# A two-block network on one core: in its second kind of layer the attention heads' values become the stationary operand, two heads share a bank by halves, and each head's probabilities are scaled before they are turned

## The chip, the core and the metric

The kernel runs on one core of a Trainium2 chip. The metric is the device time of one execution in microseconds (us). A core has a matmul engine, TensorE (PE in the profile; PEld is its weight load), VectorE (DVE), ScalarE (ACT), GpSimd (POOL) and SyncE (SP), which here only starts transfers. The engines run on their own and meet at semaphores. TensorE writes its results to eight banks of PSUM, 128 partitions by 512 numbers of 32 bits each.

## The reference, cut to what matters

`x` has 256 rows of 1024 numbers. Two layers of a first kind come first, then two layers of a second kind; the change touches the second kind alone. A layer of the second kind, shortened:

```python
h = rms_norm_2(x, g_mix)
(a_q, a_k, a_v, b_qlat, b_kvlat, b_krope, c_q, c_k, c_v, c_f, d_val, d_gate) = jnp.split(h @ w_in, ...)
out_a = chunk_band_attention(...)            # 4 heads of 64, a bias by distance, masked by chunks of 64
q = (rms_norm_2(b_qlat, g_q_lat) @ w_uq)     # the "latents": 256 and 128 numbers a row
kv = (rms_norm_2(b_kvlat, g_kv_lat) @ w_ukv)
out_b = block_causal_attention(...)          # 4 heads of 96 (values 64), with a rotation of q and k
out_c = block_causal_attention(...)          # 4 heads of 64, with a cumulated forget term
out_d = silu(layer_norm(conv(d_val * sigmoid(d_gate))))   # 31 taps
# in each head: p = softmax(scores); out = p @ v   (256 queries, 256 keys, 64 values; keys behind a query only)
proj = einsum('bsnc,ncd->bsnd', [out_a, out_b, out_c, out_d], w_branch)   # 4 branches of 256
x = x + sum(sigmoid(h @ w_gate + b_gate) * proj) @ w_o
x = x + square(relu(rms_norm_2(x, g_ffn) @ w_up)) @ w_down
```

## The kernel before

**The large products.** Weights come from memory in *slabs* of four blocks of 128 x 512 (some of two or one). ScalarE rounds a slab to `w_hi` (L1066) and VectorE takes the rest to `w_lo` (L1588); activations are split alike. Each product is three matmuls, hi by hi, hi by lo and lo by hi (L513 to L515). VectorE and ScalarE work three slabs ahead of TensorE. A product gathers in one of two pairs of banks (0 and 1, or 2 and 3). They are taken in turn by *block number*: block n waits in `open_block` until block n-2 has been read out.

**The attention beside them.** The heads of the second kind (0 to 3 are `out_a`, 4 to 7 `out_c`, 8 to 11 `out_b`) are worked on in steps. Each engine has a generator `side()`, and the table `PLAN2` says after which slab a step of it is taken. It is the same table for all engines, so the order on each is fixed by hand. In step h TensorE makes the scores of head h (`head_scores`, L847 and L848, into bank 6), turns q and k of a later pair of heads for h from 4 to 9 (`turn_head`), turns the probabilities of head h-1 (`turn_probs`) and makes the outputs of head h-2 (`head_values`, L870 to L872). Turning is a transpose on TensorE against the identity `cst` (L559 for all), into bank 4 or 5 in turn, and ScalarE copies the result out.

VectorE adds the bias and finds the rows' maxima (`soften`, L1919 to L1925), and ScalarE takes the exponentials and their sums (`exponentials`, L1385). The probabilities stay unscaled. Both have a 128 x 128 piece for the first 128 queries and a 128 x 256 piece for the others.

**The heads' outputs.** `head_values(h)` has the turned probabilities `softT2` as the stationary operand, 128 x 128, and 64 columns of values as the moving one, three matmuls in f32. Four heads fill bank 7, queries in the partitions. Then VectorE divides by the sums and writes `branch` (`normalise`, L1933 and L1936), TensorE turns `branch` with four transposes (`turn_branch`), ScalarE rounds the result to `obT_hi` and VectorE takes `obT_lo`; the products with `w_branch` (named B0 to B7) read these two. The convolution's branch goes through `turn_branch` as well. This happens for branch 0 (heads 0 to 3), 1 (4 to 7), 2 (8 to 11) and 3 (convolution).

**The latents' products.** U0 and U1 (the products with `w_uq` and `w_ukv`) stand behind gate product G0. U0 takes banks 0 and 1, and then a block number is left out, so that the number of blocks in a layer is even. U1 therefore takes banks 0 and 1 too, when ScalarE has read U0 out. At the end of the layer a number of the turning banks is left out as well. GpSimd rotates parts of q and k for heads 8 to 11 behind U1 (L2272 to L2285).

A matmul of f32 operands shows as two records in the trace, each with its own weight load; a transpose, and a matmul of the rounded operands, shows as one.

Of the kernel before, what the change touches and what calls it, by code (L numbers as in the profile page):

```python
# [21 lines left out]
F32 = mybir.dt.float32  # L22
# [6 lines left out]
P = 128  # L29
# [37 lines left out]
BLOCKS1, BLOCKS2 = 7 + 2 + 11 + 2, 5 + 2 + 16 + 2 + UPS + 2 + 1  # L67
TURNS1, TURNS2 = 4 + 4 + 4 + 4 + 4 + 4 + 4 + 11 + 4 + 1, 2 + 1 + 1 + 10 + 12 + 4 + 1 + 4 + 4 + 4 + 1
assert not (BLOCKS1 % 2 or BLOCKS2 % 2 or TURNS1 % 2 or TURNS2 % 2)
# [71 lines left out]
STEPS_DVE1, STEPS_DVE2 = 27, 87  # L141
# [51 lines left out]
def build(nc, t, out):  # L193
    with ExitStack() as ctx:
# [140 lines left out]
        probs = sem("probs")  # L335
        heads_out = sem("heads_out")
        decay_arg = sem("decay_arg")
# [154 lines left out]
        def _(pe):  # L492
# [329 lines left out]
            q.next("probs", DEPTH * DH)  # L822
            for l in q.layers(dict(slab=len(KTS2), blk=BLOCKS2, turn=TURNS2, scores=12, pool=2, dve=6, hid=UPS,
                                          probs=12, conv=1, out=3),
                              dict(turn=3)):
# [29 lines left out]
                def head_values(h):  # L855
                    pe.wait_ge(turn_free, group["probs", h] + 2)
                    if h % 4 == 0:
                        pe.wait_ge(out_free, q.next("out"))
                    if h == 0:
                        read_out(projection[3])  # L860
                    s = softT2[:, h % 2, :]

                    def v(kt):
# [40 lines left out]
                def side():  # L904
# [22 lines left out]
                    turn_branch(0)  # L927
# [6 lines left out]
                    turn_branch(2)  # L934
# [7 lines left out]
                    turn_branch(3)  # L942
# [23 lines left out]
                for name in PRODUCTS:  # L966
# [3 lines left out]
                    elif name[0] == "U":  # L970
                        pe.wait_ge(turn_free, group["latents"] + 2)
                        product(open_block(), lat_hi, lat_lo, ((0, 1), (2,))[n], (384, 512)[n], True, True)
                        if n == 0:
                            q.next("blk")
                    else:
                        pe.wait_ge(turn_free, group["branch", n // 2] + 2)
# [52 lines left out]
                for b in range(2):  # L1029
                    a = open_block()  # L1030
                    for n in range(8):
# [6 lines left out]
                        if b == 1 and n == 1 and l < DEPTH - 1:  # L1038
                            turn_added(skip=1)
# [3 lines left out]
        def _(act):  # L1043
# [296 lines left out]
            per2 = dict(slab=len(KTS2), used=len(KTS2), blk=BLOCKS2, turn=TURNS2, soft=12, act_job=1,  # L1340
                        rstd=4, squares=5, conv=1, hid=UPS, step=STEPS_ACT2,
                        **{f"in{s}": 16 * len(KTS2) // RING for s in range(RING)})
            for l in q.layers(per2, dict(slab=AHEAD, turn=3, **{f"in{s}": 16 for s in range(AHEAD)})):
# [12 lines left out]
                def take_block(dst, cols, scales, n, blocks=1):  # L1356
# [6 lines left out]
                    ins.then_inc(acc_free, blocks)  # L1363
                    q.next("blk", blocks - 1)
# [45 lines left out]
                def heads(first, end):  # L1410
                    for h in range(first, end + 2):
                        if h == 10:
                            take_hi(obT_hi[0][:, :, :])
# [18 lines left out]
                def side():  # L1432
# [15 lines left out]
                    take_hi(obT_hi[0][:, :, :])  # L1448
# [4 lines left out]
                    take_hi(obT_hi[1][:, :, :])  # L1453
# [25 lines left out]
                def latent_product(n):  # L1479
# [3 lines left out]
                    take_block(dst, (384, 512)[n], lat[n], 1, 2 - n)  # L1483
# [62 lines left out]
                if l < DEPTH - 1:  # L1546
                    take_model((0, 1), l * 16 + 48)
                    take_model((2, 3), l * 16 + 48, skip=1)
# [22 lines left out]
        def _(dve):  # L1571
# [320 lines left out]
            for l in q.layers(dict(slab=len(KTS2), used=len(KTS2), row=1, blk=BLOCKS2, turn=TURNS2,  # L1892
                                          turn_hi=2 + 4 + 4 + 4 + 4, squares=5, rstd=4, act_done=10, hid=UPS, scores=12,
                                          heads=3, layer_in=64, bgate0=64, bgate1=64, step=STEPS_DVE2),
                              dict(slab=AHEAD, turn=3, turn_hi=2)):
# [15 lines left out]
                def lo_of(dst, hi):  # L1911
                    dve.wait_ge(turn_free, q.now("turn") + 2)
                    take_lo(dst, hi)

# [13 lines left out]
                def normalise(n):  # L1928

                    dve.wait_ge(heads_out, q.next("heads"))  # L1930
                    rs, rc = (stat[:, at:at + 24].rearrange("p (r h) -> p r h", r=R)[:, :, 4 * n:4 * n + 4]
                              for at in (S_RS2, S_RC2))
                    step(dve.reciprocal(rc, rs))  # L1933
                    for r in range(R):
                        at = S_RC2 + 12 * r + 4 * n
                        ins = dve.tensor_tensor(branch[:, r, :].rearrange("p (h d) -> p h d", d=HD),  # L1936
# [397 lines left out]
```

## Time and profile before

| | |
|---|---|
| three runs, median (lowest to highest) | 1453.38 us (1453.35 to 1453.61) |
| the profiled execution | 1453.64 us |
| its span, first to last instruction | 1451.9 us |
| TensorE busy | 1438.1 us, 99% |
| VectorE, ScalarE, GpSimd busy | 932.0, 747.5, 98.4 us |
| mean granted clock of TensorE | 0.998 of 2.4 GHz |

1.7 us of the profiled time lie outside the span. The two layers of the second kind take the second half: their attention stands at about 665 to 810 us and again some 401 us later, with the same pattern. On TensorE a record's duration says little, since matmuls overlap in its pipeline. What one costs is the distance between the *starts* of neighbouring rows of the timeline; this is how the rows below are to be read.

### The profile page before, as it was taken

The page shows a single profiled execution, that of the slowest core. Times are in us where ns is not written, and L with a number is a line of the kernel's source. Part 1 is how long each engine was busy: PE and PEld are TensorE (multiplying, and loading weights), DVE is VectorE, ACT ScalarE, POOL GpSimd, SP SyncE. Part 2 cuts the span into 40 slices and gives each one's busy share as a digit, 9 for nine tenths or more (in the row PEclk, how much of TensorE's full clock was granted, in tenths as well). Part 3 has the DMA queues.
Part 4 walks back from the last instruction along what each step waited for, and adds up shares of the span by engine and source line. Part 5 has one row for each costly group of instructions (what it writes and reads, how often), then busy time and mean ns, then how long its engine had stood idle before and what let it go on. Part 6 is the DMA issues. An engine that isn't in the chain of part 4 may idle for free.

```text
span 1451.9 us, 19158 instructions
## 1 busy us (share of the span) xinstructions
PE 1438.1 (99%) x7099; PEld 1201.0 (83%) x7099; DVE 932.0 (64%) x1111; ACT 747.5 (51%) x994; POOL 98.4 (7%) x116
## 2 busy tenths in 40 slices
PE   9999999999999999999999999999999999999997
PEld 7788888888788888888888888888888888888886
DVE  6766655446756555446688878754466888787642
ACT  6765544445855444346665446543366654565441
POOL 1211000002111000000220000000002200000001
PEclk9999999999999999999999999999999999999999
DMA  8533665555435665555454566555553545665550
GB/s 333 173 123 112 231 189 190 177 183 164 149 109 170 205 186 176 182 180 186 138 177 160 187 206 211 191 193 183 174 186 118 187 160 182 217 204 190 188 186 29
DMA packets 172646, 257.12 MB, mean 177 GB/s; under 512 B 8477, under 2 KB 90399, under 8 KB 172447
## 3 DMA queue, kind: packets, MB, share of 16 engines
q1 hardware_dynamic: 169408, 249.36, 51.5%
q10 hardware_dynamic: 3023, 6.28, 1.4%
q8 instruction: 46, 0.75, 0.2%
q0 software_dynamic: 144, 0.52, 0.1%
q14 instruction: 25, 0.20, 0.0%
HBM read 255.08 MB, written 1.05 MB: 176 GB/s over the span
## 4 chain that ended last, share of the span: by engine, by line
PE 95%; DVE 2%; ACT 1%; issue 1%; DMA 0%; POOL 0%; POOLq 0%; DVEq 0%; ACTq 0%
PE bank L513 23%; PE bank L515 23%; PE bank L514 23%; PE bank L1002 8%; PE bank L559 5%; PE bank L1001 4%; PE bank L697 1%; PE bank L542 1%; PE bank L544 1%; PE bank L543 1%; PE bank L848 1%; DVE w_lo L1588 1%; PE bank L654 1%; PE bank L1004 1%; PE bank L847 1%
## 5 line engine op out<-in xcount | busy, mean ns | idle before, releaser
L1588 DVE TENSOR_TENSOR w_lo<-w_raw,w_hi 128x2048 fp32r<-128x2048 f32 (+2 forms) x247 | 538.6, 2185 | 217.4 <-ACT w_hi L1066 214.3
L1066 ACT CAST w_hi<-w_raw 128x2048 fp32r<-128x2048 f32 (+2 forms) x247 | 448.5, 1825 | 218.5 <-PE bank L515 194.7
L513 PE MATMUL bank<-w_hi,hT 128*128 128x512 f32 (+1 forms) x1056 | 417.5, 395 | 0.0
L515 PE MATMUL bank<-w_hi,hT 128*128 128x512 f32 (+1 forms) x1056 | 410.7, 389 | 0.0
L514 PE MATMUL bank<-w_lo,hT 128*128 128x512 f32 (+1 forms) x1056 | 410.0, 388 | 0.0
L515 PEld LDWEIGHTS bank<-w_hi,hT 128*128 128x128 f32 x1056 | 198.2, 188 | 41.2
L513 PEld LDWEIGHTS bank<-w_hi,hT 128*128 128x128 f32 x1056 | 198.4, 188 | 39.2 <-issue 1.5
L514 PEld LDWEIGHTS bank<-w_lo,hT 128*128 128x128 f32 x1056 | 198.6, 188 | 37.9
L1002 PE MATMUL bank<-hT,w_hi 128*128 128x512 f32 x512 | 178.2, 396 | 0.2
L1001 PE MATMUL bank<-hT,w_lo 128*128 128x256 f32 x448 | 125.2, 279 | 0.0
L2213 POOL TENSOR_TENSOR stat<-stat,cst 128x2 f32<-128x2 f32 (+4 forms) x24 | 46.4, 1935 | 967.4 <-DVE stat L1637 830.7
L1002 PEld LDWEIGHTS bank<-hT,w_hi 128*128 128x128 f32 x512 | 94.4, 188 | 21.0 <-DVE sum L2143 0.9
L513 PE MATMUL bank<-w_hi,hid2T_hi 128*128 128x512 f32 x240 | 93.5, 390 | 0.0
L515 PE MATMUL bank<-w_hi,hid2T_lo 128*128 128x512 f32 x240 | 93.4, 389 | 0.0
L514 PE MATMUL bank<-w_lo,hid2T_hi 128*128 128x512 f32 x240 | 93.4, 389 | 0.0
L1001 PEld LDWEIGHTS bank<-hT,w_lo 128*128 128x128 f32 x448 | 84.4, 188 | 1.3
L513 PE MATMUL bank<-w_hi,hid1T_hi 128*128 128x512 f32 x176 | 69.1, 392 | 0.0
L515 PE MATMUL bank<-w_hi,hid1T_lo 128*128 128x512 f32 x176 | 68.6, 390 | 0.0
L514 PE MATMUL bank<-w_lo,hid1T_hi 128*128 128x512 f32 x176 | 68.5, 389 | 0.0
L1089 ACT CAST hid1T_hi<-bank 128x512 f32 (+1 forms) x22 | 12.9, 587 | 90.3 <-PE bank L559 90.3
L1617 DVE SCALAR_TENSOR_TENSOR hT<-bank,gcols,hT 128x256 fp32r<-128x256 f32 (+1 forms) x72 | 32.6, 507 | 40.8 <-ACT hT L1096 35.5
L1525 ACT COPY cross<-bank 128x256 f32<-128x256 f32 x64 | 20.8, 378 | 70.7 <-PE bank L1002 70.7
(277 smaller groups left out, 1630.5 us busy)
## 6 DMA issues: line engine op xcount, KB each, us to landing
w_raw<-in_w_gate SPq DMA_DIRECT2D x108, 512.0 KB, 3.8
w_raw<-in_w_up SPq DMA_DIRECT2D x108, 512.0 KB, 4.6
w_raw<-in_w_down SPq DMA_DIRECT2D x104, 512.0 KB, 4.5
w_raw<-in_w_in SPq DMA_DIRECT2D x88, 512.0 KB, 4.6
w_raw<-in_w_out SPq DMA_DIRECT2D x16, 512.0 KB, 4.1
w_raw<-in_w_branch SPq DMA_DIRECT2D x32, 256.0 KB, 2.8
w_raw<-in_w_o SPq DMA_DIRECT2D x16, 512.0 KB, 4.5
bgate<-in_b_gate ACTq DMA_DIRECT2D x16, 256.0 KB, 3.3
```

What stands on the lines that cost most here:

```text
L513: pe.matmul(o, hi[:, kt, rows_of(r)], w_hi[:, s, j, 0:cols], start=begin, stop=False)
L514: pe.matmul(o, hi[:, kt, rows_of(r)], w_lo[:, s, j, 0:cols], start=False, stop=False)
L515: mm = pe.matmul(o, lo[:, kt, rows_of(r)], w_hi[:, s, j, 0:cols], start=False, stop=end)
L542: pe.matmul(a[r][:, :], hT_hi[:, kt, rows_of(r)], w_hi[:, s, j, :], start=begin, stop=False)
L559: tr = pe.transpose(b[0:m, col:col + n], src, ident[0:n, 0:n])
L1001: pe.matmul(o[:, 0:SEQ], lo[:, kt, cols], hT_hi[:, kt, :], start=False, stop=False)
L1002: mm = pe.matmul(o[:, :], hi[:, kt, cols], hT[:, :, kt, :], start=kt == 0, stop=kt == KT - 1)
L1066: act.copy(w_hi[:, s, 0:kts, :], w_raw[:, s, 0:kts, :]).then_inc(hi_ready, 1)
L1525: ins = act.copy(cross2[:, n, :], a[n][:, SEQ:2 * SEQ])
L1588: dve.tensor_tensor(w_lo[:, s, 0:kts, :], w_raw[:, s, 0:kts, :], w_hi[:, s, 0:kts, :].bitcast(F32), ALU.subtract).then_inc(lo_ready, 1)
L1617: return dve.scalar_tensor_tensor(lo, src, gain, hi.bitcast(F32), ALU.mult, ALU.subtract)
L2213: pool.tensor_tensor(dst, src, half[:, 0:n], ALU.pow).then_inc(rstd_ready, 1)
```

## The change

Four edits, all in layers of the second kind.

1. `head_values` becomes `pair_values`, taken at every odd step for two heads. The values of a head, 128 x 64, are stationary and the turned probabilities move: 256 columns for the first 128 keys (all queries) and 128 columns for the others (later queries). The even head of a pair writes partitions 0 to 63 of bank 7 and the odd one partitions 64 to 127. So bank 7 holds the branch already turned, and `turn_branch` is gone for the three attention branches; ScalarE (`take_branch`) and VectorE (`lo_of_branch`) read bank 7 itself. The convolution's branch is still turned (`turn_conv`).
2. Queries now lie along the columns, so a head can't be divided by its sums behind the product. `scale_probs` (VectorE) multiplies the probabilities before they are turned, one head at a time: a reciprocal and two `tensor_scalar`. `turn_probs` waits for it (`scaled` in place of `probs`). It stands behind the step's slab split, for head 3 ahead of `latents`. `normalise` is gone.
3. In a step `pair_values` stands ahead of `turn_probs`; `head_values` stood behind it.
4. No block number and no turning number is left out: U1 takes banks 2 and 3, and all later blocks the other pair than before.

```diff
-BLOCKS1, BLOCKS2 = 7 + 2 + 11 + 2, 5 + 2 + 16 + 2 + UPS + 2 + 1
+BLOCKS1, BLOCKS2 = 7 + 2 + 11 + 2, 5 + 2 + 16 + 2 + UPS + 2
...
                 def turn_probs(h):
-                    pe.wait_ge(probs, q.next("probs"))
+                    pe.wait_ge(scaled, q.next("scaled"))
...
-                    o = [score[1][:, r * BW + (h % 4) * HD:r * BW + (h % 4 + 1) * HD] for r in range(R)]
-                    pe.matmul(o[0], s[:, 0:P], v(0), start=True, stop=True)
-                    pe.matmul(o[1], s[:, P:2 * P], v(0), start=True, stop=False)
-                    mm = pe.matmul(o[1], s[:, 2 * P:3 * P], v(1), start=False, stop=True)
+                    for kt, at, n in ((0, 0, SEQ), (1, 2 * P, P)):
+                        for e in range(2):
+                            mm = pe.matmul(score[1][e * HD:(e + 1) * HD, (c + 1) * SEQ - n:(c + 1) * SEQ],
+                                           v(h - 1 + e, kt), softT2[:, e, at:at + n], start=kt == 0, stop=kt == 1)
...
-                def turn_branch(n):
-
-                    pe.wait_ge(out_free, q.now("out") + 1)
-                    group["branch", n] = turn_group([(branch[:, r, c * P:(c + 1) * P], c * SEQ + r * P)
-                                for c in range(2) for r in range(R)])
...
                     for h in range(first, end + 2):
-                        if h == 10:
-                            turn_branch(1)
                         if h < end:
                             head_scores(h)
                             if 4 <= h < 10:
                                 turn_head(h)
+                        if h >= first + 2 and h % 2:
+                            pair_values(h - 2)
                         if first < h <= end:
                             turn_probs(h - 1)
-                        if h >= first + 2:
-                            head_values(h - 2)
...
                         product(open_block(), lat_hi, lat_lo, ((0, 1), (2,))[n], (384, 512)[n], True, True)
-                        if n == 0:
-                            q.next("blk")
...
+                def take_branch(dst):
+
+                    act.wait_ge(heads_out, q.next("heads"))
+                    act.copy(dst[:, :, :], score[1][:, :].rearrange("p (c n) -> p c n", n=SEQ)).then_inc(branch_hi, 1)
...
-                def normalise(n):
-
-                    dve.wait_ge(heads_out, q.next("heads"))
-                    rs, rc = (stat[:, at:at + 24].rearrange("p (r h) -> p r h", r=R)[:, :, 4 * n:4 * n + 4]
-                              for at in (S_RS2, S_RC2))
-                    step(dve.reciprocal(rc, rs))
...
+                def scale_probs(h):
+
+                    dve.wait_ge(probs, q.next("probs"))
+                    rs, rc = (stat[:, at:at + 24].rearrange("p (r h) -> p r h", r=R)[:, :, h] for at in (S_RS2, S_RC2))
+                    step(dve.reciprocal(rc, rs))
+                    for r, (a, z) in enumerate(((0, P), (P, 3 * P))):
+                        ins = dve.tensor_scalar(soft2[:, h % 2, a:z], soft2[:, h % 2, a:z], rc[:, r:r + 1], None, ALU.mult)
+                    ins.then_inc(scaled, 1)
...
+                def lo_of_branch(n):
+
+                    dve.wait_ge(branch_hi, q.next("branch_hi"))
+                    dve.tensor_tensor(obT_lo[n][:, :, :], score[1][:, :].rearrange("p (c n) -> p c n", n=SEQ),
+                                      obT_hi[n][:, :, :].bitcast(F32), ALU.subtract).then_inc(out_free, 1)
...
                     if s not in (12, 38):
                         splits(1)
+                    while softened:
+                        scale_probs(softened.pop(0))
                     if s >= TAPS_FROM:
```

TensorE's queue in step 3 of the first attention, before (scores of head 3, probabilities of head 2 turned, outputs of head 1; bank 7 takes the outputs):

```order
L847 MATMUL bank6<-qkT2_77 128x128 [waits turn_free,scores_out]
L848 MATMUL bank6<-qkT2_77 128x256
L559 MATMUL bank5<-cst,soft2_78 128x128 [waits turn_free,probs]
L559 MATMUL bank5<-cst,soft2_78 128x128 x2
L870 MATMUL bank7<-p_b_65,softT2_79 128x64 [waits turn_free]
L871 MATMUL bank7<-p_b_65,softT2_79 128x64
L872 MATMUL bank7<-p_b_65,softT2_79 128x64
```

And with the change (the outputs are those of heads 0 and 1; line 874 is the matmul in `pair_values`):

```order
L848 MATMUL bank6<-qkT2_77 128x128 [waits turn_free,scores_out]
L849 MATMUL bank6<-qkT2_77 128x256
L874 MATMUL bank7<-softT2_79,p_b_65 64x256 [waits acc_free,out_free,turn_free]
L874 MATMUL bank7<-softT2_79,p_b_65 64x256
L874 MATMUL bank7<-softT2_79,p_b_65 64x128 x2
L561 MATMUL bank5<-cst,soft2_78 128x128 [waits turn_free,scaled]
L561 MATMUL bank5<-cst,soft2_78 128x128 x2
```

The four matmuls of a pair stand between scores and transposes, and step 2 ahead of this one has no outputs to make.

TensorE's queue between U0 and U1, before (`branch` is the transposes of branch 0, `cqa` and `cka` those of heads 4 and 5, `lat_hi` the latents):

```order
L515 MATMUL bank1<-w_hi,lat_lo_69 128x384
L559 MATMUL bank4<-cst,branch_75 128x128 [waits turn_free,out_free]
L559 MATMUL bank4<-cst,branch_75 128x128 x3
L559 MATMUL bank5<-cst,cqa_85 66x128 [waits turn_free,dve_ready,pool_ready]
L559 MATMUL bank5<-cst,cqa_85 66x128
L559 MATMUL bank5<-cst,cka_86 66x128 x2
L513 MATMUL bank0<-w_hi,lat_hi_68 128x512 [waits lo_ready,acc_free,turn_free]
```

And with the change:

```order
L517 MATMUL bank1<-w_hi,lat_lo_69 128x384
L561 MATMUL bank4<-cst,cqa_85 66x128 [waits turn_free,dve_ready,pool_ready]
L561 MATMUL bank4<-cst,cqa_85 66x128
L561 MATMUL bank4<-cst,cka_86 66x128 x2
L515 MATMUL bank2<-w_hi,lat_hi_68 128x512 [waits lo_ready,acc_free,turn_free]
```

The four transposes are gone, and U1 opens bank 2 instead of bank 0.

VectorE's queue around steps 8 and 9, before (`w_lo` are slab splits, `yT` taps of the convolution, `mix2` a branch product read out):

```order
L1925 TENSOR_REDUCE stat<-soft2_78 128x1
L1588 TENSOR_TENSOR w_lo<-w_raw,w_hi 128x2048 [waits hi_ready]
L2060 SCALAR_TENSOR_TENSOR yT_88<-uT_87,ccols,yT_88 128x256 [waits dve_step] x3
L2097 SCALAR_TENSOR_TENSOR mix2_70<-gate2_64,bank0 128x512 [waits act_done,slab_used]
L2097 SCALAR_TENSOR_TENSOR mix2_70<-gate2_64,bank1 128x512
L1919 SCALAR_TENSOR_TENSOR soft2_78<-bank6,cst 128x384 [waits scores]
```

And with the change:

```order
L1924 TENSOR_REDUCE stat<-soft2_78 128x1
L1591 TENSOR_TENSOR w_lo<-w_raw,w_hi 128x2048 [waits hi_ready]
L1931 RECIPROCAL stat<-stat 128x2 [waits probs]
L1933 TENSOR_SCALAR soft2_78<-soft2_78,stat 128x128 [waits dve_step]
L1933 TENSOR_SCALAR soft2_78<-soft2_78,stat 128x256
L2060 SCALAR_TENSOR_TENSOR yT_88<-uT_87,ccols,yT_88 128x256 [waits dve_step] x3
L2096 SCALAR_TENSOR_TENSOR mix2_70<-gate2_64,bank2 128x512 [waits act_done,slab_used]
```

The three instructions of `scale_probs` stand between the slab split and the taps, and the taps and the reading of banks are queued behind their wait.

## Rows read from the trace of the kernel before

**Rows 1.** The page: busy time of TensorE, and the chain that ended last.

```profile
PE 1438.1 (99%) x7099; PEld 1201.0 (83%) x7099; DVE 932.0 (64%) x1111; ACT 747.5 (51%) x994; POOL 98.4 (7%) x116
PE 95%; DVE 2%; ACT 1%; issue 1%; DMA 0%; POOL 0%; POOLq 0%; DVEq 0%; ACTq 0%
```

**Rows 2.** Timeline, TensorE, head 10's values: start, us, engine, line, operation, shapes, count.

```profile
784.96 0.49 PE L559 MATMUL bank<-cst,soft 128*128 128x128 f32 x3
785.29 0.33 PE L870 MATMUL bank<-kvB,softT 128*128 128x64 f32 x2
...
786.19 0.39 PE L514 MATMUL bank<-w_lo,hT 128*128 128x512 f32 x1
```

**Rows 3.** Groups by form, TensorE: records, busy us, mean ns, idle.

```profile
L559 PE MATMUL bank<-cst,branch 128*128 128x128 f32 x32 | 4.8, 272 | 0.0
...
L872 PE MATMUL bank<-p_b,softT 128*128 128x64 f32 x16 | 3.1, 275 | 0.0
```

**Rows 4.** Timeline, TensorE, between U0 and U1.

```profile
720.03 0.60 PE L559 MATMUL bank<-cst,branch 128*128 128x128 f32 x4
...
720.68 0.38 PE L559 MATMUL bank<-cst,cka 128*66 128x128 f32 x2
721.43 0.47 PE L513 MATMUL bank<-w_hi,lat_hi 128*128 128x512 f32 x1 [0.37 <-issue]
721.74 0.40 PE L514 MATMUL bank<-w_lo,lat_hi 128*128 128x512 f32 x1
```

**Rows 5.** Timeline, TensorE, step 5: scores over 66 rows, transposes, next slab.

```profile
730.33 0.38 PE L847 MATMUL bank<-qkT 66*128 66x128 f32 x2
730.55 0.60 PE L848 MATMUL bank<-qkT 66*128 66x256 f32 x2
730.99 0.38 PE L559 MATMUL bank<-cst,cqa 128*66 128x128 f32 x2
...
731.43 0.49 PE L559 MATMUL bank<-cst,soft 128*128 128x128 f32 x3
...
731.99 0.39 PE L514 MATMUL bank<-w_lo,hT 128*128 128x512 f32 x1
```

**Rows 6.** Timeline, TensorE, step 3: scores over 64 rows.

```profile
697.51 0.48 PE L847 MATMUL bank<-qkT 64*128 64x128 f32 x2
697.83 0.59 PE L848 MATMUL bank<-qkT 64*128 64x256 f32 x2
698.36 0.55 PE L559 MATMUL bank<-cst,soft 128*128 128x128 f32 x3
```

**Rows 7.** Timeline, TensorE, first kind: scores from both row halves.

```profile
50.80 0.39 PE L514 MATMUL bank<-w_lo,hT 128*128 128x512 f32 x1
51.03 0.39 PE L515 MATMUL bank<-w_hi,hT 128*128 128x512 f32 x1
51.35 1.14 PE L654 MATMUL bank<-qkT 64*128 64x256 f32 x8
52.42 0.66 PE L559 MATMUL bank<-cst,proj 128*128 128x128 f32 x4
```

**Rows 8.** Tile soft, VectorE: duration ns min/median/max.

```profile
L1744 DVE TENSOR_SCALAR comb<-soft,stat x16: 346/350/355, 62.8 to 397.4; 128x256 f32<-128x256 f32 x16
```

**Rows 9.** Timeline, VectorE, `normalise(0)`.

```profile
718.80 0.19 DVE L1933 RECIPROCAL stat<-stat 128x8 f32<-128x8 f32 x1
719.03 0.76 DVE L1936 TENSOR_TENSOR branch<-bank,stat 128x256 f32<-128x256 f32 x2
```

**Rows 10.** Timeline, three engines, head 8: split, last exponential, transposes.

```profile
757.75 2.28 DVE L1588 TENSOR_TENSOR w_lo<-w_raw,w_hi 128x2048 fp32r<-128x2048 f32 x1
...
759.60 0.19 ACT L1385 ACTIVATION_READ_ACCUMULATOR soft<-soft,stat 128x1 f32 x1
...
761.07 0.49 PE L559 MATMUL bank<-cst,soft 128*128 128x128 f32 x3
```

**Rows 11.** Windows: each engine's busy us in the stretch, clock, DMA.

```profile
725.00:745.00 20.00, 20.00 (x102) 16.84 (x101) 18.39 (x28) 15.70 (x27) 8.30 (x16) 1.00 0.63 203
```

More of the change, by code:

```diff
@@ L140 @@
 STEPS_ACT1, STEPS_ACT2 = 4, 8
-STEPS_DVE1, STEPS_DVE2 = 27, 87
+STEPS_DVE1, STEPS_DVE2 = 27, 96
 STEPS_POOL1, STEPS_POOL2 = 0, 24
@@ L335, in build @@
         probs = sem("probs")
+        scaled = sem("scaled")
         heads_out = sem("heads_out")
+        branch_hi = sem("branch_hi")
         decay_arg = sem("decay_arg")
@@ L821, in _ @@
             pe.wait_ge(consts_in, 16)
-            q.next("probs", DEPTH * DH)
             for l in q.layers(dict(slab=len(KTS2), blk=BLOCKS2, turn=TURNS2, scores=12, pool=2, dve=6, hid=UPS,
-                                          probs=12, conv=1, out=3),
-                              dict(turn=3)):
+                                          scaled=12, conv=1, out=3),
+                              dict(turn=2)):
                 projection = [q.now("blk") + n for n in range(len(COLS2) + 3)]
@@ L972, in _ @@
                         product(open_block(), lat_hi, lat_lo, ((0, 1), (2,))[n], (384, 512)[n], True, True)
-                        if n == 0:
-                            q.next("blk")
-                    else:
-                        pe.wait_ge(turn_free, group["branch", n // 2] + 2)
+                    else:
+                        if n < 6:
+                            pe.wait_ge(out_free, group["branch", n // 2] + 1)
+                        else:
+                            pe.wait_ge(turn_free, group["conv"] + 2)
                         at = OUT_OF[n // 2]
@@ L1338, in _ @@
                 block_of()
-            per2 = dict(slab=len(KTS2), used=len(KTS2), blk=BLOCKS2, turn=TURNS2, soft=12, act_job=1,
+            per2 = dict(heads=3, slab=len(KTS2), used=len(KTS2), blk=BLOCKS2, turn=TURNS2, soft=12, act_job=1,
                         rstd=4, squares=5, conv=1, hid=UPS, step=STEPS_ACT2,
                         **{f"in{s}": 16 * len(KTS2) // RING for s in range(RING)})
-            for l in q.layers(per2, dict(slab=AHEAD, turn=3, **{f"in{s}": 16 for s in range(AHEAD)})):
+            for l in q.layers(per2, dict(slab=AHEAD, turn=2, **{f"in{s}": 16 for s in range(AHEAD)})):
                 ahead = iter(KTS2[AHEAD:] + KTS2[:AHEAD])
@@ L1362, in take_block @@
                         ins = act.activation(dst(r), a[r][:, 0:cols], ACT.Copy, scale=scales[r])
-                    ins.then_inc(acc_free, blocks)
-                    q.next("blk", blocks - 1)
+                    ins.then_inc(acc_free, 1)
                 def load_gate_bias(u):
@@ L1892, in _ @@
             for l in q.layers(dict(slab=len(KTS2), used=len(KTS2), row=1, blk=BLOCKS2, turn=TURNS2,
-                                          turn_hi=2 + 4 + 4 + 4 + 4, squares=5, rstd=4, act_done=10, hid=UPS, scores=12,
-                                          heads=3, layer_in=64, bgate0=64, bgate1=64, step=STEPS_DVE2),
-                              dict(slab=AHEAD, turn=3, turn_hi=2)):
+                                          turn_hi=2 + 1 + 4 + 4 + 4, squares=5, rstd=4, act_done=10, hid=UPS, scores=12,
+                                          probs=12, branch_hi=3, layer_in=64, bgate0=64, bgate1=64, step=STEPS_DVE2),
+                              dict(slab=AHEAD, turn=2, turn_hi=2)):
                 ahead = iter(KTS2[AHEAD:] + KTS2[:AHEAD])
@@ L1975, in heads @@
                             step(dve.tensor_scalar(z, z, 0.0, None, ALU.min))
-                        if h in (9, 13):
-                            normalise((h - 5) // 4)
                         yield
@@ L2001, in side @@
                     yield from heads(0, 4)
-                    normalise(0)
                     b = next_turn()
@@ L2077, in latent_product @@
                     others(1)
-                    q.next("blk", 1 - n)
                 def gate(u):
@@ L2116, in _ @@
                 root()
-                attention, convolution = side(), taps()
+                attention, convolution, softened = side(), taps(), []
                 for s in range(40):
@@ L2278, in _ @@
                     rotate(r, a, b, a, b, False)
-                pool.wait_ge(acc_free, q.next("blk", 4) + 2)
+                pool.wait_ge(acc_free, q.next("blk", 3) + 2)
                 for r in range(R):
@@ L2289, in _ @@
                 root_x()
-                q.next("blk", BLOCKS2 - 9)
+                q.next("blk", BLOCKS2 - 8)
             pool.wait_ge(lo_ready, RING + DEPTH * (len(KTS1) + len(KTS2)))
```

55 lines of the change are left out of this document (25 added, 30 removed).

## Prediction

> **What bounds the kernel now.** I read the page first, then TensorE's timeline in the attention. On the page TensorE is busy 1438.1 of 1451.9 us and has 95% of the chain that ended last, while VectorE is busy 64% and ScalarE 51% [rows 1]. So the end is set by how many microseconds of instructions TensorE's queue holds. A microsecond taken out of that queue is a microsecond off the time, as long as no other engine comes late; one taken from VectorE or put on it is worth nothing while it stays hidden. The timeline then gives what each small piece costs. The reader is to take differences of starts: two neighbouring slab matmuls of 512 columns start 0.23 us apart (50.80 to 51.03 in [rows 7]); that is the unit in what follows.
>
> **What goes.** *Values.* In head 10's step three transposes start at 784.96 and the values at 785.29, 0.33 later, so a transpose is 0.11. From the values' start to the second matmul of the slab behind them (786.19) it is 0.90; 0.23 of that is the slab's own first matmul, so a head's values cost 0.67 us [rows 2]. That is six records at 0.11 each: 64 moving columns cost as much as 128 (below), so weight loads, not columns, set their pace. The trace has nine groups of 16 such records, one of them in [rows 3], so 144 records or 24 heads: 24 x 0.67 = 16.1 us.
>
> *Transposes of the branches.* The first four start at 720.03, and the `cka` row, the seventh and eighth, at 720.68: 0.65 for six [rows 4]. So one is 0.11 and a group of four 0.44. 32 records are there [rows 3], of which 8, the convolution's, stay: 24 x 0.11 = 2.6 us. Nothing else hangs on them, since ScalarE and VectorE took their output before and now take bank 7 in their stead, with instructions of one shape.
>
> *The block number.* The last two transposes start at 720.68 and should be done 0.22 later. The second matmul of U1 starts at 721.74; with 0.45 (0.22 and one slab matmul) it would be 721.13. The row of U1's first matmul shows 0.37 of that as idle [rows 4]. 0.61 us are lost, because bank 0 has not been read out. In banks 2 and 3 U1 waits for the reading of G0, which ended a whole product (U0) earlier. Nothing else in the steady state waits there, and the numbers behind U1 keep their distance of two. Two layers: 1.2 us. The left-out turning number cost nothing, since its bank had been read a product before.
>
> Together 16.1 + 2.6 + 1.2 = 19.9 us.
>
> **What comes on TensorE: 12 pairs.** No matmul of the kernel before has an output of 64 partitions, so this is bounded from nearby rows.
>
> *Columns.* Per head 256 and 128 moving columns. With f32 operands two records of 128 columns take 0.22 (730.33 to 730.55) and two of 256 take 0.44 (730.55 to 730.99) [rows 5]. So one head's stream is 0.66 us, and a pair's is 0.66 if the two halves of the array run side by side and 1.32 if they don't. The nearest row for that is in the first kind: eight records of 256 columns over 64 rows, four on partitions 0 to 63 and four on 64 to 127, start at 51.35 and the next piece starts at 52.42 [rows 7]. One behind the other they would need 8 x 0.22 = 1.76 us; they took 1.07. Halves of the rows do run side by side. Here it is halves of the columns, into one bank, and both streams are read from the same 128 partitions; I take the same.
>
> *Going into and out of halves.* Those 1.07 are 0.19 above 4 x 0.22, and the start is late by 0.09 (0.32 from 51.03 instead of 0.23) [rows 7]. The scores over 64 rows show the same: 0.32 and 0.53 [rows 6] where scores over 66 rows need 0.22 and 0.44 [rows 5], 0.19 more. With some 0.05 for what follows, a piece in halves costs 0.33 us beyond its columns. The Trainium skill says the same in words (TensorEngine Tiling (Array Packing), Key Properties: changing the tiling mode drains the engine). This rule speaks against the change, and the rows give it a size. A pair is then 0.66 + 0.33 = 1.0 us. Two of the twelve (heads 0 and 1 of each layer) follow scores that are in halves already, where one side is paid: 0.9. Sum 10 x 1.0 + 2 x 0.9 = 11.8 us. Both ends: no cost of switching at all gives 12 x 0.66 = 7.9, columns one after the other with switching 12 x 1.65 = 19.8.
>
> On columns the skill has a figure (TensorE: Matmul & The Clock Gate, Part 3): three column tiles ran 2.38 times as fast as one after the other. If two column tiles kept the same part of their speed (2.38 of 3, so 1.59 of 2), a pair would be 1.32 / 1.59 + 0.33 = 1.16 us by an estimate from that page, and the sum -6.2 us. No row of this trace shows column tiles, and the sum here stands on the row halves alone.
>
> **What comes elsewhere.** *VectorE.* A head's scaling is a reciprocal with its wait, 0.23 (718.80 to 719.03 [rows 9]), and two products with a column of `stat`. The same instruction on 128 x 256 takes 0.35 with its fill [rows 8]. So it is 0.7 to 0.9 us a head and 17 to 22 us in all; the six `normalise`, 0.99 each by rows 9 (718.80 to 719.79), go. 11 to 16 us more on an engine that is idle for a third of the time: nothing, if the places are right. The fullest stretch is 725 to 745, 18.39 of 20 busy [rows 11], where three heads add 2.3; the `normalise` that stood just ahead of it gives 1.0 back, and the 1.6 us idle take the rest. Slab splits are three slabs ahead and bear such a shift. Without that cover the price would be the 11 to 16 us.
>
> *The new wait.* `turn_probs(h)` now waits for VectorE as well. What is queued behind it on TensorE is the slab, and so everything. The tightest place is head 8, whose next slab is a short one. VectorE's split ends at 757.75 + 2.28 = 760.03, the exponentials at 759.79, so the scaling would end at 760.7 to 760.9; the transposes started at 761.07 [rows 10]. In the changed order outputs of a pair (1.0) stand ahead of them and those of one head (0.67) are gone, which gives 0.3 more. Slack 0.5 us: no wait. For most heads a slab of 24 matmuls, 24 x 0.23 = 5.5 us, lies between scores and transposes. In VectorE's own queue the scaling stands behind the split, when the exponentials are done; only head 3's does not, but VectorE waited for ScalarE's squares there anyhow.
>
> *ScalarE and GpSimd* keep their instructions. GpSimd's rotations hang on U1, which comes earlier by as much as their reader does.
>
> **Sum.** 11.8 - 19.9 = -8.1 us. The profiled execution took 1453.64 (span 1451.9 and 1.7 around it), 0.26 above the median of the three runs; 1453.38 - 8.1 = 1445.3 us.
>
> **The rivals.** 0.2% (2.9 us) is about what a measurement of this kernel can tell from no change.
>
> *A. The halves run side by side*, as summed: 1445.3. For it: the row halves [rows 7]. Its own range is 1442 (switching nearly free: 7.9 - 19.9 = -12.0) to 1448 (0.2 more a pair). Chance 0.70.
>
> *B. The column halves run one after the other*, since both streams come from the same partitions. A pair is 1.32 + 0.33 = 1.65, twelve are 19.6, and the change gives 0.3: 1453.1, no difference. Against it: nothing in the trace but that it was never done there. Chance 0.13.
>
> *C. The scaling comes late.* If `scaled` comes 1 us late for head 8 (a short slab) and head 4 (its scores stand where VectorE is fullest), in two layers, it takes back 4 us: 1449.4. Rows 10 have 0.5 us for it, rows 11 say where VectorE is full. Chance 0.10.
>
> *D. Slower: each change of half drains the array.* The four matmuls of a pair go half 0, half 1, half 0, half 1, so beyond B there are three more changes of 0.19 us, and a pair is 2.2: 12 x 2.2 = 26.6, 6.7 us slower, 1460.1. It decides from 1.66 us a pair, where gain and loss are equal. Against it: in rows 7 the halves were changed within the group and the extra was 0.19 for all of it. Chance 0.05. The last 0.02 are for what I don't see.
>
> **The numbers.** Faster by over 0.2%: A and C, 0.80. Within: B and what of C goes further, 0.13. Slower: 0.07 with D. The forecast is A's. Its range alone holds 0.65, with C 0.75, so the range reaches to B: 1442.5 to 1453.5.
>
> **What would show it.** The records of the new matmul: for a pair, 0.9 to 1.0 us from its first start to the next piece beyond the slab's, records of both halves starting within hundredths of each other. If they start 0.22 apart, B. Between U0 and U1 no idle row. The three instructions of the scaling with 0.7 to 0.9 us a head, and no wait on TensorE that names them; if there is one, C, and it should be at heads 4 or 8. TensorE's busy time down by some 7 us and the span with it. Wrong I would be above all through the one thing with no row, column halves from the same partitions.

## The result and the profile after

The changed kernel takes 1446.38 us (median of four runs, 1446.28 to 1447.69), the kernel before beside it 1453.49 (1453.35 to 1453.71). The ratio is 0.995 with a 95% interval of 0.9938 to 0.9961, so 7.1 us less (5.7 to 9.0 by the interval) where 8.1 were forecast.

Executions of a kernel fall mostly in two groups some 1.4 us apart, and the difference arises in the first 20 us, ahead of the changed layers: the transposes of `x` behind the first slabs start at 16.39 to 16.82 us in six of the eleven profiles, that of the kernel before among them, and at 18.02 to 18.31 in the other five, with that of the changed kernel.

```profile
16.82 1.04 PE L559 MATMUL bank<-cst,x 128*128 128x128 f32 x8
```

```profile
18.15 1.04 PE L561 MATMUL bank<-cst,x 128*128 128x128 f32 x8
```

(Timeline of TensorE, kernel before and kernel after: start, us, engine, line, operation, shapes, count.) So the two spans, 1451.9 and 1445.9, differ by 6.0 us and not by 7.1 or more. Differences of less than a microsecond are therefore taken from places inside the traces, from the first layer of the second kind on. Beside the median of an experiment stands its lowest run, to be held against the lowest ones of the kernel before (1453.2 in each experiment's series) and of the changed kernel (1446.3).

From the page of the changed kernel, busy times and the chain, beside [rows 1]:

```profile
PE 1432.6 (99%) x7027; PEld 1189.1 (82%) x7027; DVE 942.3 (65%) x1165; ACT 746.4 (52%) x994; POOL 100.7 (7%) x116
PE 93%; DVE 2%; ACT 1%; POOL 1%; issue 1%; DMA 0%; POOLq 0%; DVEq 0%; ACTq 0%
```

TensorE is still the bound. It is busy 5.5 us less, where some 7 were forecast; the later start of this profile hides about 1 us of the difference (eight matmuls of `ones` around 11 us took 2.02 us instead of 1.11). VectorE is busy 10.3 more, below the 11 to 16 forecast. GpSimd, with the same 116 instructions, is busy 2.3 more and stands in the chain with 1% now.

The step of head 3 in the timeline of TensorE, to be read beside [rows 6]:

```profile
698.46 0.59 PE L849 MATMUL bank<-qkT 64*128 64x256 f32 x2
698.98 0.87 PE L874 MATMUL bank<-softT,p_b 128*64 128x256 f32 x8
699.78 0.55 PE L561 MATMUL bank<-cst,soft 128*128 128x128 f32 x3
700.17 0.60 PE L561 MATMUL bank<-cst,p_b 128*128 128x128 f32 x4
700.90 0.44 PE L561 MATMUL bank<-cst,p_c 128*128 128x128 f32 x2
701.09 0.44 PE L515 MATMUL bank<-w_hi,hT 128*128 128x420 f32 x1
```

A pair, eight records, takes 0.80 us from its start to the next piece (698.98 to 699.78). Side by side its columns need 0.66 by the prediction, one after the other 1.32 without any switching. So A, and not B or D. Further down something unforeseen stands: four transposes of `p_b` start at 700.17, and those of `p_c` 0.73 later. In the kernel before it was 0.44 (699.36 to 699.80). They start when ScalarE's copy of the turned probabilities has ended, at 700.85:

```profile
700.37 0.48 ACT L1377 COPY softT<-bank 128x384 f32<-128x384 f32 x1 [3.08 <-PE bank L561]
```

Between U0 and U1, beside [rows 4]:

```profile
721.09 0.38 PE L561 MATMUL bank<-cst,cka 128*66 128x128 f32 x2
721.23 0.48 PE L515 MATMUL bank<-w_hi,lat_hi 128*128 128x512 f32 x1
721.54 0.40 PE L516 MATMUL bank<-w_lo,lat_hi 128*128 128x512 f32 x1
...
722.92 0.38 PE L561 MATMUL bank<-cst,cka 128*66 128x128 f32 x2
723.27 0.46 PE L848 MATMUL bank<-qkT 66*128 66x128 f32 x2
```

The second matmul of U1 starts 0.45 after `cka`, as forecast, and no row shows idle time.

**Where the gain lies.** How far the start of the slab behind each step moves, after less before, in the first layer of the second kind (the second repeats the numbers within 0.04):

| place | forecast, us | measured |
|---|---|---|
| four even steps, which only lose a head's values (heads 2, 4, 8 and 12 in the loop) | -0.67 each | -0.65 to -0.69 |
| six steps with a pair for one head | +0.24, then +0.33 each | +0.53, then +0.27 to +0.35 |
| transposes of the first branch and the wait of U1 | -1.04 | -1.04 |
| head 10: values and transposes of the second branch | -1.11 | -1.11 |
| transposes of the third branch | -0.44 | -0.44 |
| head 4's scores, behind U1 | 0 | -0.24 |
| head 5's step | 0 | +0.14 |
| head 6's step, which loses values too | -0.67 | -0.32 |
| layer | -4.05 | -3.6 |

Twice -3.6 is -7.2, close to the medians' 7.1. The forecast was right nearly line by line. Three small waits (in the steps of heads 3, 5 and 6) cost 1.6 us of it in the two layers; an earlier start at head 4 gave 0.5 back and the other ten pairs 0.3.

### The profile page after: what moved, and what is told of

Same layout as the page of the kernel before. It is cut to its first block, busy times and chain, and to the rows that moved or that the text cites. A ratio compares the mean times of both kernels' runs of the same rounds, so it can differ in the third digit from the quotient of the medians.

```text
span 1445.9 us, 19056 instructions
## 1 busy us (share of the span) xinstructions
PE 1432.6 (99%) x7027; PEld 1189.1 (82%) x7027; DVE 942.3 (65%) x1165; ACT 746.4 (52%) x994; POOL 100.7 (7%) x116
## 3 DMA queue, kind: packets, MB, share of 16 engines
HBM read 255.08 MB, written 1.05 MB: 177 GB/s over the span
## 4 chain that ended last, share of the span: by engine, by line
PE 93%; DVE 2%; ACT 1%; POOL 1%; issue 1%; DMA 0%; POOLq 0%; DVEq 0%; ACTq 0%
PE bank L515 23%; PE bank L517 23%; PE bank L516 23%; PE bank L1001 8%; PE bank L561 4%; PE bank L1000 4%; PE bank L699 1%; POOL cst L2273 1%; PE bank L544 1%; PE bank L546 1%; PE bank L545 1%; PE bank L874 1%; DVE w_lo L1591 1%; PE bank L656 1%; ACT w_hi L1065 1%
```

## The experiments

**1. Each head's values alone.** The same 48 matmuls, but each head's at its own step:

```diff
-                        if h >= first + 2 and h % 2:
-                            pair_values(h - 2)
+                        if h >= first + 2:
+                            half_values(h - 2)
...
+                    e = h % 2
                     for kt, at, n in ((0, 0, SEQ), (1, 2 * P, P)):
-                        for e in range(2):
-                            mm = pe.matmul(score[1][e * HD:(e + 1) * HD, (c + 1) * SEQ - n:(c + 1) * SEQ],
-                                           v(h - 1 + e, kt), softT2[:, e, at:at + n], start=kt == 0, stop=kt == 1)
+                        mm = pe.matmul(score[1][e * HD:(e + 1) * HD, (c + 1) * SEQ - n:(c + 1) * SEQ],
+                                       v(h, kt), softT2[:, e, at:at + n], start=kt == 0, stop=kt == 1)
```

> The changed kernel, but each head's values are issued at that head's own step instead of a pair of heads together: the same 48 matmuls, shapes and destinations, never two heads side by side. Theory (the two halves of a bank are filled side by side, so a second head of a pair is nearly free): a head alone costs what a pair's streams cost, about 0.63 us, plus the 0.33 us of switching, 24 times 0.96 = 23.0 us against 12 times 0.99 = 11.9 us of the pairs: about +11 us over the changed kernel, 1457.5 us. Rival (a head's own streams cost half of the pair's 0.66 us, one behind the other, and nothing runs side by side): 24 times (0.33 + 0.33) = 15.8 us, about +4 us, 1450.4 us. Rival that the switching is not paid a second time: +7.5 us, 1454 us.

Measured: 1457.92 us (lowest 1456.93), in the trace 10.9 us more than the changed kernel: 0.79 to 0.96 in each step that now has a group of its own, 0.91 in the mean. One head alone, from its timeline of TensorE:

```profile
699.91 0.86 PE L874 MATMUL bank<-softT,p_b 128*64 128x256 f32 x4
700.70 0.55 PE L561 MATMUL bank<-cst,soft 128*128 128x128 f32 x3
```

Four records take 0.79 us, where eight took 0.80. A second head on the other half costs 0.01. Grouping decides the change: with single heads it would be some 3.5 us slower than the kernel before (interval of the ratio 1.0014 to 1.0033).

**2. The order within a pair.** Both matmuls of the first head ahead of both of the second:

```diff
-                    for kt, at, n in ((0, 0, SEQ), (1, 2 * P, P)):
-                        for e in range(2):
+                    for e in range(2):
+                        for kt, at, n in ((0, 0, SEQ), (1, 2 * P, P)):
```

> The changed kernel, but in each pair both matmuls of the first head (256 and 128 columns) are issued ahead of both of the second, instead of in turn. Theory (matmuls start in the order in which they are written, and only neighbours on different halves overlap): the 256 of the first head run alone (0.43 us), its 128 beside the start of the second head's 256 (0.43), then the second head's 128 (0.21): 1.07 against 0.64 us a pair, 12 times +0.43 = +5.1 us, 1451.5 us. Rival (each half has a queue of its own, and the order written does not matter): no change, 1446.4 us. Rival (no overlap at all once the order is this): +0.64 times 12 = +7.7 us, 1454 us.

Measured: 1446.36 us, no change; my theory fell. Two answers of the trace for the line of the pairs in a window of 0.06 us at a group's start (records, duration in ns as min/median/max, first and last start), first for this kernel from 697.50 on, then for experiment 1 from 699.90 on:

```profile
L874 PE MATMUL bank<-softT,p_b x2: 430/430/430, 697.5 to 697.5; 128*64 128x256 f32 x2
```

```profile
L874 PE MATMUL bank<-softT,p_b x1: 430/430/430, 699.9 to 699.9; 128*64 128x256 f32 x1
```

A head alone has one record of 256 columns under way there, its second comes later; here there are two at once. So the second is the other head's: its matmul was issued third and started ahead of the second, one of 128 columns. A matmul doesn't wait here for one issued earlier on the other half. This holds if the queue has the order in which the kernel is written, and no listing of this run's queue was kept; for it speaks that in the traces' records the two halves' first ones start 14 ns apart here and 7 ns in the changed kernel, where their matmuls are neighbours.

**3. The pairs issued twice**, so that a pair's streams are priced without the switching:

```diff
-                    for kt, at, n in ((0, 0, SEQ), (1, 2 * P, P)):
+                    for _, kt, at, n in [(i, *x) for i in range(2) for x in ((0, 0, SEQ), (1, 2 * P, P))]:
```

> The changed kernel with the four matmuls of each of the 12 pairs issued twice in a row (the second time they overwrite the first with the same values), so that the added time is a pair's streams alone, without the switching to and from the half-width shape. Theory (two streams side by side, 0.64 us a pair by the 256 + 128 columns, and the switching of 0.33 us once a pair as before): 12 times 0.64 = +7.7 us over the changed kernel, 1454.1 us. Rival (the streams of the halves share time, and 0.66 us was made up of something else): 12 times 1.28 = +15.4 us, 1461.8 us. Rival (each return to the first columns pays the switching again): 12 times 0.97 = +11.6 us, 1458.0 us.

Measured: 1453.64 us (lowest 1453.56), +7.3 over the changed kernel or 0.61 a pair. The trace is more exact, since in the whole time some small waits absorb a part. Its timeline of TensorE, for the pair of heads 4 and 5:

```profile
747.73 1.52 PE L874 MATMUL bank<-softT,p_c 128*64 128x256 f32 x16
749.18 0.33 PE L561 MATMUL bank<-cst,soft 128*128 128x128 f32 x1
```

Sixteen records take 1.45 us to the next piece, in every pair of the trace 1.45 or 1.46, where eight take 0.80. So a pair's streams are 0.65 us, against 0.66 in the prediction. A group of its own costs 0.91 by experiment 1 and a pair 0.94 to 1.02 by the table (0.67 of values gone, and 0.27 to 0.35 more). What is left for switching is 0.26 to 0.37, against 0.33.

**4. The block number alone**, on the kernel before:

```diff
-BLOCKS1, BLOCKS2 = 7 + 2 + 11 + 2, 5 + 2 + 16 + 2 + UPS + 2 + 1
+BLOCKS1, BLOCKS2 = 7 + 2 + 11 + 2, 5 + 2 + 16 + 2 + UPS + 2
...
                         product(open_block(), lat_hi, lat_lo, ((0, 1), (2,))[n], (384, 512)[n], True, True)
-                        if n == 0:
-                            q.next("blk")
```

> The kernel before with one part of the change alone: the first product of the latents leaves no block number out, so that the second one writes the other bank. Theory: the wait of 0.61 us between the two products goes, once in each of the two layers of the second kind, and nothing behind it waits instead: -1.2 us, 1452.3 us. Rival (the time is lost again at the next wait, for the rotations on GpSimd or for the copies on ScalarE): less than 0.3 us, 1453.3 us.

Measured: 1454.48 us (lowest 1453.11; ratio 1.0, 0.9991 to 1.0009): nothing. Its timeline of TensorE says why; the rows of the kernel before stand behind it:

```profile
721.97 0.38 PE L559 MATMUL bank<-cst,cka 128*66 128x128 f32 x2
722.11 0.47 PE L513 MATMUL bank<-w_hi,lat_hi 128*128 128x512 f32 x1
...
724.22 0.41 PE L559 MATMUL bank<-cst,cqa 128*66 128x128 f32 x2 [0.47 <-DVE obT_lo L1610]
724.46 0.38 PE L559 MATMUL bank<-cst,cka 128*66 128x128 f32 x2
724.98 0.46 PE L847 MATMUL bank<-qkT 66*128 66x128 f32 x2
```

```profile
722.93 0.41 PE L559 MATMUL bank<-cst,cqa 128*66 128x128 f32 x2
723.18 0.38 PE L559 MATMUL bank<-cst,cka 128*66 128x128 f32 x2
723.69 0.46 PE L847 MATMUL bank<-qkT 66*128 66x128 f32 x2
```

The wait between U0 and U1 is gone, and the next transposes wait instead, for VectorE's reading of the turned branch. With 1.3 us of later start taken off, L847 stands where it stood (724.98 and 723.69). In the changed kernel this reader is gone: a branch is no longer turned, so its reading holds no turning bank. The rival was right that the time is lost again at the next wait, but neither GpSimd nor ScalarE, which it named, sets that wait: VectorE does.

**5. The block number left out again**, in the changed kernel (the edit of experiment 4 the other way round):

> The changed kernel with one part undone: the first product of the latents leaves a block number out again, so that both write the same bank. The kernel before with this part alone gained nothing, since the next wait, for VectorE's read of the turned branch, took the 0.61 us over; in the changed kernel that reader is gone. Theory (the two waits stood one behind the other, and only both parts together take them away): TensorE waits 0.61 us again between the two products and makes it up nowhere, twice 0.61 = +1.2 us over the changed kernel, 1447.6 us. Rival (the number is worth nothing in either kernel): 1446.4 us.

Measured: 1446.95 us (lowest 1446.67), and in the trace +0.36 and +0.38 us in the two layers, 0.7 in all. TensorE waits even 1.04 longer between the products (0.61, and the 0.44 of the four transposes that no longer fill the wait), but then the steps of heads 4, 5 and 6 give back 0.20, 0.13 and 0.35:

```profile
719.70 0.38 PE L561 MATMUL bank<-cst,cka 128*66 128x128 f32 x2
720.88 0.47 PE L515 MATMUL bank<-w_hi,lat_hi 128*128 128x512 f32 x1 [0.80 <-issue]
...
736.50 0.60 PE L849 MATMUL bank<-qkT 66*128 66x256 f32 x2
736.93 0.38 PE L561 MATMUL bank<-cst,qB 128*96 128x128 f32 x2
```

Behind the longer wait the transposes of `qB` start 0.43 after the scores; in the changed kernel that gap is 0.74 (experiment 7). Whoever comes later waits less for the others. Neither the theory nor the rival had the size: the number is worth 0 alone, 0.7 us beside the rest of the change, and 1.2 only if nothing else waits behind it.

**6. The scaling alone**, on the kernel before (`scale_probs` as in the changed kernel, and TensorE waiting for it):

```diff
-                    pe.wait_ge(probs, q.next("probs"))
+                    pe.wait_ge(scaled, q.next("scaled"))
...
-                    step(dve.reciprocal(rc, rs))
                     for r in range(R):
-                        at = S_RC2 + 12 * r + 4 * n
-                        ins = dve.tensor_tensor(branch[:, r, :].rearrange("p (h d) -> p h d", d=HD),
-                                                score[1][:, r * BW:(r + 1) * BW].rearrange("p (h d) -> p h d", d=HD),
-                                                stat[:, at:at + 4].unsqueeze(2).to_broadcast([P, 4, HD]), ALU.mult)
+                        ins = dve.tensor_copy(branch[:, r, :], score[1][:, r * BW:(r + 1) * BW])
```

> The kernel before with one part of the change alone: VectorE scales each head's probabilities ahead of their transposes, and the scaling of a branch becomes a plain copy of the same size. Theory: VectorE's extra 0.74 us a head lies beside TensorE's work save at heads 4 and 8, where the scaled probabilities come up to 0.1 us late: between 0 and +0.6 us in all, 1453.7 us. Rival (the scaling comes late in most heads, or VectorE's extra work slows GpSimd's rotations so that the transposes of the third kind of heads wait for them): +2 to +4 us, 1456 us.

Measured: 1454.33 us (lowest 1452.70; ratio 0.9997, 0.9988 to 1.0006), and in the trace 0.24 us *less* a layer, all of it at head 4's scores: `normalise` has lost its reciprocal (0.23 by [rows 9]), so VectorE reads the turned branch earlier. No head's transposes came late. VectorE's 0.74 us a head are hidden, as forecast. From the timeline of VectorE in the changed kernel, head 4's probabilities:

```profile
730.22 0.17 DVE L1931 RECIPROCAL stat<-stat 128x2 f32<-128x2 f32 x1
730.42 0.61 DVE L1933 TENSOR_SCALAR soft<-soft,stat 128x128 f32<-128x128 f32 x2
730.96 1.60 DVE L2060 SCALAR_TENSOR_TENSOR yT<-uT,ccols,yT 128x256 f32<-128x256 f32 x3
```

The scaling ends at 731.03 and TensorE's transposes start at 731.09, 0.31 after the two ahead of them instead of 0.22. That is most of the 0.14 at head 5's step in the table: rival C, at 0.1 us instead of 1.

**7. Probabilities ahead of the rotated parts** in head 6's step, on TensorE and ScalarE:

```diff
-                            if 4 <= h < 10:
+                            if 4 <= h < 10 and h != 6:
                                 turn_head(h)
...
                             turn_probs(h - 1)
+                        if h == 6:
+                            turn_head(h)
```

> The changed kernel, but in the step of head 6 the transposes of head 5's probabilities stand ahead of those of the rotated queries and keys, on TensorE and on ScalarE. Theory: the transposes of the rotated parts wait 0.31 us for GpSimd's last copy in each layer; 0.25 us of other work ahead of them fills that, 2 times -0.25 = -0.5 us, 1445.9 us. Rival (GpSimd comes later by as much, or the head behind waits for its keys instead): no change, 1446.4 us.

Measured: -0.34 and -0.32 us in that step of the two layers, nothing elsewhere; 1446.79 us (lowest 1445.31). The last copy of GpSimd and then TensorE's rows in the changed kernel:

```profile
737.37 0.49 POOL L2286 COPY kB<-p_c 128x128 f32<-128x128 f32 x1
...
737.17 0.60 PE L849 MATMUL bank<-qkT 66*128 66x256 f32 x2
737.91 0.42 PE L561 MATMUL bank<-cst,qB 128*96 128x128 f32 x2
```

and with the order changed:

```profile
737.32 0.60 PE L849 MATMUL bank<-qkT 66*128 66x256 f32 x2
737.75 0.49 PE L561 MATMUL bank<-cst,soft 128*128 128x128 f32 x3
738.08 0.38 PE L561 MATMUL bank<-cst,qB 128*96 128x128 f32 x2
```

GpSimd's copy ends at 737.86 and TensorE goes on at 737.91. The transposes of the probabilities fill the gap. So my sentence that the rotations come earlier by as much as their reader does was wrong.

**8. The first pair behind the transposes of head 2's probabilities**, which get a place of their own:

```diff
+        softT3 = over("softT3", [P, 384], 31.5)
...
-                        if h >= first + 2 and h % 2:
+                        if h >= first + 2 and h % 2 and h != 3:
                             pair_values(h - 2)
                         if first < h <= end:
                             turn_probs(h - 1)
+                        if h == 3:
+                            pair_values(h - 2)
```

> The changed kernel, but the values of heads 0 and 1 stand behind the transposes of head 2's probabilities, as in the kernel before, and so ahead of the transposes of the latents; head 2's turned probabilities have a place of their own for it. Theory: in the changed kernel the last transposes of the latents wait some 0.3 us in each layer for ScalarE's copy of the turned probabilities; with the pair's 0.8 us between them this wait goes, 2 times -0.3 = -0.6 us, 1445.8 us. Rival (the pair's own wait or switching takes its place): no change, 1446.4 us.

Measured: -0.21 us in each layer, 1445.87 us (lowest 1445.26). From its timeline of TensorE:

```profile
697.53 0.55 PE L562 MATMUL bank<-cst,soft 128*128 128x128 f32 x3
698.01 0.87 PE L875 MATMUL bank<-softT,p_b 128*64 128x256 f32 x8
698.81 0.66 PE L562 MATMUL bank<-cst,p_b 128*128 128x128 f32 x4
699.30 0.38 PE L562 MATMUL bank<-cst,p_c 128*128 128x128 f32 x2
```

The 0.73 between `p_b` and `p_c` is 0.49 now. Part of it comes back as switching: the scores over 64 rows are no longer the pair's neighbour (the transposes take 0.48 up to the pair, not 0.39). The theory was right, the size 0.4 instead of 0.6.

**9. Both orders at once** (the diffs of 7 and 8).

> The changed kernel with both changes of order at once: the values of heads 0 and 1 behind the transposes of head 2's probabilities, and the transposes of head 5's probabilities ahead of those of the rotated queries and keys. Theory: the two waits stand in different steps and add up, -0.5 - 0.6 = -1.1 us against the changed kernel, 1445.3 us, some 8.2 us under the kernel before. Rival (GpSimd's chain hangs on work that comes earlier by less than its reader, so that its wait grows by what the first part saves): -0.6 us, 1445.8 us.

Measured: 1445.27 us (1445.02 to 1446.63; ratio to the kernel before 0.9943, interval 0.993 to 0.9957), in the trace -0.21 and -0.34, then -0.21 and -0.32, together -1.1 us against the changed kernel. The waits are independent and add up. This is the fastest of the versions.

## Why the prediction held, step by step

- **The bound.** TensorE's queue set the end, and time taken from it was time gained but for the waits above. Right.
- **Values and transposes that go.** -0.67 a head and -0.44 a group of four: measured -0.65 to -0.69 and -0.44. Right.
- **The pairs.** Side by side: right, as forecast from the row halves, though both streams come from the same partitions; experiment 1 shows a second head at 0.01 us. Streams 0.65 and switching 0.26 to 0.37 by experiments 1 and 3 and the table; forecast 0.66 and 0.33. B and D fell. The lower end of A's own range, 1442, should have read 1441.4 by its own sum (1453.38 - 12.0); nothing hangs on it. The estimate from the Trainium skill (TensorE: Matmul & The Clock Gate, Part 3, column tiles at 2.38 of 3) was 1.16 us a pair; a pair measured 0.94 to 1.02 here, and the two halves overlap in full; the measurement decides. Its rule that changing the tiling mode drains the engine (TensorEngine Tiling (Array Packing), Key Properties) agrees with the 0.26 to 0.37 us; changing the half within a group cost nothing visible.
- **The block number**, -1.2. The place was read rightly and the wait did go, but the term isn't one of its own. The step that failed is "nothing else in the steady state waits there": alone it gives nothing, because VectorE's reading of the turned branch waits behind it (experiment 4), and within the change it is worth 0.7 (experiment 5).
- **"Nothing else hangs on them"** (the transposes). Wrong in our favour: their turning bank, held until VectorE had read it, held up head 4's scores. With them gone these come 0.24 us earlier, and the block number becomes worth something.
- **VectorE's scaling**: hidden, 0.74 us a head for 0.7 to 0.9. Head 8 had no wait. Head 4 had one of 0.1 us.
- **The order around `turn_probs`.** I asked who is queued behind the new wait, not what its new place does to the turning banks. Placed directly ahead of the latents' transposes, it makes these wait for ScalarE's copy: 0.29 us a layer more than forecast, of which another order gets back 0.21 (experiment 8).
- **GpSimd** "earlier by as much as their reader": wrong. In the changed kernel its chain from the first product to the last copy took 10.68 us (727.18 to 737.86), in the kernel before 9.42 (727.61 to 737.03), with the same instructions. With the scaling alone it was 9.87 (728.51 to 738.38). So VectorE's extra work beside it lengthens it, by 0.45. The other 0.8 us of the whole change stand in the first four products, 3.30 us instead of 2.50, and nearly all of it in the very first: 1.05 us instead of 0.33. It is the one that starts while VectorE is still in a slab split. Start of the products and the split beside them, kernel before and then changed kernel:

```profile
727.61 2.50 POOL L2272 TENSOR_TENSOR cst<-qB,rope 128x64 f32<-128x64 f32 x4 [12.72 <-ACT kvB L1362]
725.38 2.29 DVE L1588 TENSOR_TENSOR w_lo<-w_raw,w_hi 128x2048 fp32r<-128x2048 f32 x1
```

```profile
727.18 3.30 POOL L2273 TENSOR_TENSOR cst<-qB,rope 128x64 f32<-128x64 f32 x4 [11.25 <-ACT kvB L1361]
725.77 2.28 DVE L1591 TENSOR_TENSOR w_lo<-w_raw,w_hi 128x2048 fp32r<-128x2048 f32 x1
```

GpSimd starts 0.06 us before the split's end in the one (727.67) and 0.87 before it in the other (728.05). The other kept traces go with this: in experiments 4 and 6 it starts 0.07 before the end and the four take 2.50, in experiments 1, 3 and 5 0.86 to 0.87 before it and they take 3.30. No run moved the split alone, so the cause is well supported but not tested apart.

Summed for the two layers: -8.1 as forecast, +0.6 at the latents, +0.7 at GpSimd, +0.3 at head 5, -0.5 at head 4, -0.3 for the other ten pairs, +0.1 in the rest: -7.2. That the sum missed by no more than 0.9 is in part luck: what went wrong at single places was 1.6 one way and 0.8 the other.

## What to carry to other kernels

When two small outputs fit in the two halves of a bank, issue them in one group: the second is free, and it is the number of groups in halves that costs (here 0.91 us for one of its own, a second head 0.01), not the number of heads in them. Before counting a wait as a gain, look in the same stretch for the next wait on a chain of another engine; two waits in a row are worth less than their sum, and taking one alone may give nothing. And when a piece moves in the order, ask also which bank it takes and who needs the next one.

## What the runs showed of the hardware

- Two f32 streams of 256 + 128 columns each, on the two column halves and with moving data from the same 128 partitions, took 0.80 us from start to next piece; one of them alone took 0.79.
- The first matmul of the second half started 14 ns behind the first one of the other half although a further matmul of the first half stands between them in the kernel (experiment 2).
- Repeating a pair within its group added 0.65 us to the group (0.80 to 1.45); a group of its own added 0.91.
- The same 16 GpSimd instructions of the rotation span 9.42, 9.87 or 10.68 us in three kernels whose VectorE queues differ beside them. The first of them took 0.33 us when it started 0.06 us before the end of VectorE's slab split, and 1.05 when it started 0.87 before it.
